# Expert lists of a mixture-of-experts layer: a table gives each rank its slot

## The reference, cut to what matters

```python
eid = grp[:, None] * EXPERTS_PER_GROUP + top_i      # two experts for each token
e_flat, w_flat = eid.reshape(tk), gates.reshape(tk)  # tk = 2 * 520
order = jnp.argsort(e_flat)                          # rows sorted by expert
...
def expert_block(args):
    rows, e = args
    xb = h_pad[rows]
    return (jax.nn.silu(xb @ w_g[e]) * (xb @ w_u[e])) @ w_d[e]
...
contrib = y_rows[dest].astype(F32) * w_s[:, None]
out = jax.ops.segment_sum(contrib, tok_s, num_segments=t)
```

## Time and profile before

| | us |
|---|---|
| median of 3 runs | 2056.97 |
| lowest and highest | 2051.32, 2060.11 |
| the profiled execution's own time | 2054.3 |
| its span, first to last instruction | 2052.5 |
| TensorE busy | 1777.7 (87%) |
| VectorE busy | 673.2 (33%) |
| ScalarE busy | 249.5 (12%) |
| GpSimd busy | 285.8 (14%) |
| DMA queue q1 (weights and most loads) | 515.95 MB, 66.9% of the sixteen engines' span |
| DMA queue q0 (gathers and scatters of rows) | 17.12 MB, 2.5% |

### The profile page before, as it was taken

One profiled execution on the slowest core, in us unless ns is written; L12 is line 12 of the kernel. 1 busy time (PEld: TensorE's weight loads), 2 busy tenths in 40 slices (PEclk: granted clock), 3 DMA queues, 4 the chain that ended last, 5 costly groups with the idle time before them and its releaser, 6 DMA issues.

```text
span 2052.5 us, 22212 instructions
## 1 busy us (share of the span) xinstructions
PE 1777.7 (87%) x8780; PEld 1112.3 (54%) x8780; DVE 673.2 (33%) x1339; ACT 249.5 (12%) x492; POOL 285.8 (14%) x188
## 2 busy tenths in 40 slices
PE   8999999998798999996979998989877878778760
PEld 7888888886577888883334343434332323223220
DVE  6900999644663300007321212121111111111116
ACT  3003111004422011011000000000000000000002
POOL 0552232215701000001100001010000000000000
PEclk9999999999899999997999999999999999898985
DMA  5255122349743244117999999999999999999947
GB/s 236 83 129 118 69 82 77 133 175 139 31 184 140 92 154 165 64 60 313 336 411 408 407 412 399 410 399 391 391 406 396 414 401 416 402 405 411 409 177 290
DMA packets 90884, 540.66 MB, mean 263 GB/s; under 512 B 28248, under 2 KB 41048, under 8 KB 44664
## 3 DMA queue, kind: packets, MB, share of 16 engines
q1 hardware_dynamic: 77792, 515.95, 66.9%
q0 software_dynamic: 5632, 17.12, 2.5%
q10 hardware_dynamic: 7376, 6.39, 1.1%
HBM read 521.91 MB, written 31.98 MB: 270 GB/s over the span
## 4 chain that ended last, share of the span: by engine, by line
PE 56%; DMA 28%; DVE 7%; POOL 3%; ACT 2%; issue 1%; ACTq 1%; SPq 1%; DVEq 0%; POOLq 0%
PE psum L597 29%; DMA arena<-w_up_in 26%; PE psum L895 8%; PE psum L930 6%; PE psum L888 3%; PE psum L891 3%; PE psum L871 1%; ACTq L988 1%; PE psum L694 1%; SPq L512 1%; PE psum L897 1%; DMA arena<-y_rows 1%; PE psum L637 1%; DMA arena<-v_cache_in 1%; PE psum L806 1%
## 5 line engine op out<-in xcount | busy, mean ns | idle before, releaser
L597 PE MATMUL psum<-arena 128*128 128x260 f32 x3328 | 743.2, 387 | 14.8 <-DMA arena<-w_in_in 8.2
L597 PEld LDWEIGHTS psum<-arena 128*128 128x128 f32 x3328 | 639.3, 192 | 115.6 <-DMA arena<-w_in_in 8.2
L895 PE MATMUL psum<-arena 128*64 128x512 f32 x896 | 439.6, 650 | 117.1 <-DMA arena<-w_up_in 116.3
L897 PE MATMUL psum<-arena 128*64 128x512 f32 x896 | 440.4, 651 | 0.0
L895 PEld LDWEIGHTS psum<-arena 128*64 128x64 f32 x896 | 129.5, 150 | 381.4 <-issue 380.2
L930 PE MATMUL psum<-arena 128*64 128x512 f32 (+1 forms) x1024 | 258.0, 603 | 17.5 <-ACT arena L1126 17.4
L930 PEld LDWEIGHTS psum<-arena 128*64 128x64 f32 (+1 forms) x1024 | 86.5, 145 | 165.8 <-issue 142.4
L1678 DVE TENSOR_TENSOR arena<-arena,psum 64x512 f32<-64x512 f32 x28 | 19.4, 691 | 459.0 <-ACT arena L1123 459.0
L1240 POOL DMA_INDIRECT y_rows<-arena x32 | 37.0, 1156 | 929.2 <-DVE arena L1689 546.7
L897 PEld LDWEIGHTS psum<-arena 128*64 128x64 f32 x896 | 129.6, 150 | 15.3 <-issue 15.3
L1689 DVE COPY arena<-psum 64x512 f32<-64x512 f32 (+1 forms) x64 | 43.7, 688 | 254.7 <-PE psum L930 253.9
(11 more groups left out here) (321 smaller groups left out, 1308.2 us busy)
## 6 DMA issues: line engine op xcount, KB each, us to landing
arena<-w_gate_in SPq DMA_DIRECT2D x64, 2048.0 KB, 38.3
arena<-w_up_in SPq DMA_DIRECT2D x64, 2048.0 KB, 42.4
arena<-w_down_in SPq DMA_DIRECT2D x64, 2048.0 KB, 42.2
arena<-w_in_in SPq DMA_DIRECT2D x32, 1024.0 KB, 4.8
arena<-w_out_in SPq DMA_DIRECT2D x16, 1024.0 KB, 4.7
arena<-k_cache_in SPq DMA_DIRECT2D x8, 1024.0 KB, 6.7
arena<-v_cache_in SPq DMA_DIRECT2D x8, 1024.0 KB, 4.7
arena<-y_rows SPq DMA_DIRECT2D x4, 2048.0 KB, 19.2
```

The costliest lines, as they stand in the source:

```text
L597: last = mm(banks[:, h, :], w(kk), rhs(kk)[:, HALF * h:HALF * (h + 1)], start=(kk == first), stop=(kk == kn - 1 and stop))
L895: lastg = mm(ps[0:SLIM, 2, :], xt[:, 8 * hf + kk, :], wg[:, kk, :], start=(hf == 0 and kk == 0), stop=(hf == 1 and kk == 7))
L897: lastu = mm(ps[SLIM:P, 2, :], xt[:, 8 * hf + kk, :], wu[:, kk, :], start=(hf == 0 and kk == 0), stop=(hf == 1 and kk == 7))
```

## The change

Three edits, and one new function.

The constant along the slots is renamed and filled from a table: slot s of a slim block holds no longer rank s but `rank[s]`. In `ranks_of_slots`, rank r below 64 is cut into `turn`, `engine` = r // 16, r % 16 and goes to slot 4 * engine + turn // 2 + 2 * ((engine // 8 + turn) % 2). So ranks 0 to 15 fall on slots 0, 4, 8, ..., 28 and 34, 38, ..., 62, ranks 16 to 31 on 2, 6, ..., 30 and 32, 36, ..., 60. Ranks 64 to 127 keep their own place in the table. Slots 0 to 3 now hold ranks 0, 32, 16 and 48, slots 32 to 35 ranks 24, 56, 8 and 40.

For a wide block the comparison reads the table in another order: slot 8q + a gets entry 16a + q. Slots whose number modulo 8 is under 4 then hold the ranks 0 to 63, the others the ranks 64 to 127.

```diff
-        iota_b, iota_s, valid, tok, tie = col(NBLK), col(CAP), col(5), col(5), col(NE)
+        iota_b, slot_rank, valid, tok, tie = col(NBLK), col(CAP), col(5), col(5), col(NE)
...
-                tt(sel16(g), iota_s[:, 0:cap].unsqueeze(1).unsqueeze(1).to_broadcast([P, 5, b1 - b0, cap]),
-                   posblk[:, :, b0:b1].unsqueeze(3).to_broadcast([P, 5, b1 - b0, cap]),
-                   ALU.is_equal).then_inc(s_sel, 1)
+                if cap == SLIM:
+                    tt(sel16(g), slot_rank[:, 0:cap].unsqueeze(1).unsqueeze(1).to_broadcast([P, 5, b1 - b0, cap]),
+                       posblk[:, :, b0:b1].unsqueeze(3).to_broadcast([P, 5, b1 - b0, cap]),
+                       ALU.is_equal).then_inc(s_sel, 1)
+                else:
+                    tt(sel16(g).rearrange("p t b (q a) -> p (t b) q a", a=8),
+                       slot_rank.rearrange("p (a q) -> p q a", a=8).unsqueeze(1).to_broadcast([P, 5, 16, 8]),
+                       posblk[:, :, b0:b1].unsqueeze(3).to_broadcast([P, 5, 16, 8]),
+                       ALU.is_equal).then_inc(s_sel, 1)
...
+def ranks_of_slots():
+
+    import numpy as np
+    rank = np.arange(CAP)
+    for r in range(SLIM):
+        turn, engine = divmod(r, 16)
+        rank[4 * engine + turn // 2 + 2 * ((engine // 8 + turn) % 2)] = r
+    return rank
...
-    c["c_router"] = np.concatenate([np.tile(np.arange(NBLK), (P, 1)), np.tile(np.arange(1, CAP + 1), (P, 1)),
+    c["c_router"] = np.concatenate([np.tile(np.arange(NBLK), (P, 1)), np.tile(1 + ranks_of_slots(), (P, 1)),
```

## The result

| | before | changed |
|---|---|---|
| median, us | 2055.15 (4 runs) | 2035.18 (4 runs) |
| lowest to highest | 2051.32 to 2060.11 | 2025.05 to 2037.41 |
| profiled execution | 2054.3 | 2033.08 |

The ratio is 0.9889, with a 95% interval of 0.9861 to 0.9918. A second comparison, in the experiments, gave 0.9896 (0.9865 to 0.9927).

What follows compares the result with a forecast made beforehand. DMA engines, by the slowest of sixteen, were taken to bound the expert stage. −14.3 − 7 + 0.5 = −20.8 us on 2054.3 gave 2033.5, with the runs' median 2.7 above: 2036 us; forecast 2026 to 2046, range 2020 to 2056.

Steps and rivals of the forecast that it cites:

- The bound: Expert stage, 1006 to 1952 us: the DMA engines bound it at about 405 GB/s; the slowest of sixteen counts.
- Which slot lies on which engine: Slim slots 2e, 2e+1, 32+2e, 33+2e on engine e; first 64 wide slots on eight engines, eight each.
- four in a row: Rejected slim-block reading, slots 4e to 4e+3 on engine e; engines 0 and 7 would be 76 rows, 47 us, apart.
- Rows per engine: Expert gathers and scatters: slowest engine goes from 106 to 83 rows at 0.62 us each, 14.3 us less.
- Dips: DMA rate falls during slim gathers, some 38 us after 1006 us; a fifth off, −7 us.
- the bound of −38: Best case for the slim gathers: no dip at all, by the wide gathers, −38 us.
- select: Slot comparison, 0.82 us, two wide ones on the path: between 0 and +1.6 us, taken as +0.5.
- Cover: TensorE is next when DMA gets faster; its weight waits, 27 and 96.5 us, cover the gain.
- Slower: Rival: crossing lasts longer, each of 25 slim-gather dips costs 1.2 us more, +16, 2073 us; chance 0.09.
- Same: Rival: slim-gather dips grow as broad as the largest, +14, and eat the 14.3, 2057 us; chance 0.19.
- Much faster: Rival: crossing was pairs of engines writing into one group; dips fall by two thirds, 2018 us; chance 0.12.

Runs made afterwards that it cites:

- opposite table: Slim ranks 0 to 3 in slots 0, 1, 32, 33 and so on, wide blocks rank = slot, against the kernel before: 2082.44 us, 1.0125.
- spread wide blocks alone: Against the kernel before, wide blocks dealt over all sixteen engines, slim blocks keeping rank = slot: 2047.62 us, 0.9946.
- the fastest kernel: Changed kernel with slim gathers over 128 slots and wide blocks filled from slot 64 first: 1997.82 us, 0.9717 of the kernel before.

## Why the prediction was right, and where its parts were off

**The bound** was read rightly. The DMA engines set the time of the expert stage, and TensorE waited less once they were faster (19 and 89 us in place of 27 and 96.5); the last engine's end moved by 18 us, and the end of the program with it.

**Which slot lies on which engine.** Both readings held. The opposite table cost 26 us where the reading said 23.5; by "four in a row" it would have cost nothing. In the changed kernel q0 takes 40.4% of the sixteen engines in the first part of the first wide gather and 24.9% in a later one:

```profile
q0 software_dynamic: 40, 0.20, 40.4%
...
q0 software_dynamic: 20, 0.12, 24.9%
```

The second is eight engines at half their time, so eight engines still carry eight rows each, as said. The first is about thirteen, against fourteen; with the first ranks on eight engines and ranks 64 to 87 on eight others in two to four rows each that fits.

**Rows per engine, −14.3 us.** The right order of size, and the main term, but the rule behind it, time by the slowest engine's rows, is not complete. It came within 3 us in three kernels: −16 for the slim table with its dips (−15 to −17 measured), +23.5 for the opposite one (+26), −8 for spread wide blocks alone (−11). It failed in the fourth, nothing for the wide order alone, where 10 to 14 us were measured twice. The prediction said of the wide blocks that their rows gain nothing; that step failed. In the change as a whole it is worth less, 5 us, the difference between the slim table alone and both, of which 5 rows less on the slowest engine are 3.

The prediction also looked for the whole term in the idle time at the end, and took its 19 us as a cap. By the count the slowest engine lies 25 us behind the mean before (82 moves) and 11 in the changed kernel (36). The idle time at the end fell only from 19 to 12 or 13 us; 11 us of the gain lie ahead of 1925 us, 5 of them in the slim gathers. How much of the others is the slowest engine's rows, no trace tells, since it does not name the engine of a packet. The prediction also took this term and the dips as independent, and they are not: inside a dip a row costs more than 0.31 us. Around the gather of 38 rows at 1253 us, from 1252 to 1259 us, queue q0 of the kernel before reads:

```profile
q0 software_dynamic: 114, 0.35, 19.3%
```

That is 22 us of engine time for 0.35 MB, where 26.7 GB/s would make 13.

**Dips, −7 us.** The size came near: they fell from 37 to 32 us in the traces, −5. But that it was the new table that made them shallower is not borne out. The opposite table, which crowds the rows, has 31 us of them, and the wide order alone, with the old slim table, 34. Their cost hardly depends on the table, so the agreement is in part luck. That they belong to the 64-slot form was right: with 128 slots they are gone, as the bound of −38 had it. Nor did cost follow the number of rows: nine rows cost 0.6 us in the changed kernel and eighteen 0.7, where it had been 0.3 and 1.2.

**select, +0.5 us.** 1.22 us in place of 0.82, two of them on the path. TensorE waits 2.1 us for them and its weight loads 0.9, where it was 1.3 and 0.5. Some +1 us.

**Cover.** It held, as the fastest kernel shows: waits of 77 us remain after 1460 us.

The sum, −20.8 us, is what was measured (−20.0 by the medians, −21.2 by the spans). By what is left over, the terms are nearer to −16 (rows), −5 (dips) and +1, but the first of these was not measured by itself, and part of it is not explained by the count. That the total agrees to a microsecond is luck, since runs of one kernel differ by 9 to 12 us, and the range of 2020 to 2056 left room for nearly any gain; what bears the account are the experiments, the opposite table above all.

**The rivals.** "Slower", deeper dips, is out: the 18-row gather shows 367 GB/s, not under 280. "Same" is out by the ratio. "Much faster" would have come with another form of the transfer, not with this table.

## What to carry to other kernels

When DMA bounds a stage and its big transfers are split evenly over the engines, ask what the small ones do to the slowest engine: the rate after the first engine runs out comes down in steps, each step is an engine, and the length of the stairs is time to be had. Count the rows per engine from how an indirect transfer over n partitions is split, which differs between 64 and 128 partitions. And look at the rate inside each kind of small transfer, since one form may slow all engines and another, with the same rows, none.

## What the runs showed of the hardware that was not expected

A gather over 64 slots brings the sixteen engines from 425 down to between 248 (38 rows) and 350 GB/s (12 rows) for some 5 us; the same rows in a gather over 128 slots leave them at 416 to 435 GB/s. That is worth some 20 us in both kernels in which it was tried, after the price of a less even split.

With an even split and no dips, the sixteen engines hold 423 to 427 GB/s, nearly all of it float32 weights, for 900 us on end.

Left open: why the wide order alone gains 10 to 14 us, ahead of the end, while the slowest engine keeps its rows, and whether the dips are due to the ports or to something else in how 64 slots are dealt out.
